# A hybrid encoder layer on one core: loads, waits, fills and closing sums put in another order

## The chip, the cores and the metric

The kernel runs on one core of one Trainium2 chip, as one program. The time is the device time of that core in microseconds (us), from start to end of one execution. Each engine (TensorE, ScalarE, VectorE, GpSimd, SyncE) runs its own list of instructions in order, and waits on semaphores that the others or the transfers raise. A matmul reads a stationary and a moving operand from SBUF and writes to PSUM.

## The reference

One layer (DEPTH = 1) is applied to a prompt of 256 rows and a sample of 1024 rows, with D_MODEL = 1024. All is float32.

```python
def run_trunk(x, ...):
    x = x + token_mixer(rmsnorm(x, norm_mix[l]), ...)
    x = x + expert_choice_ffn(rmsnorm(x, norm_ffn[l]), w_router[l], w_gate[l], w_up[l], w_down[l])
    return rmsnorm(x, norm_final)
# token_mixer: proj = hn @ w_in; a depthwise convolution over 5 rows, SiLU and an L2 norm on the
# first 3*512 columns feed a gated delta rule in both directions; the next ones feed windowed
# attention; both are gated, summed and multiplied by w_out.
# expert_choice_ffn: each of 16 experts takes its top T/8 rows (by affinity) and computes
    hdn = silu(xe @ w_gate) * (xe @ w_up)
    y[idx] += (hdn @ w_down) * gate
```

An expert thus takes 128 sample rows and 32 prompt rows, and the last result is an RMS norm of all rows.

## The kernel before, in words

The 1280 rows are ten tiles of 128 rows. Products that need precision are made of three matmuls: both factors are split into a rounded part and a rest (`rest`, line 78), and rounded x rounded, rounded x rest and rest x rounded are added. The work goes through phases, with a barrier of all engines between two. The change touches three of them.

**`phase_norm`, 0 to 40 us.** SyncE loads the ten x tiles (line 162), the gain and the identity, and the first two of 24 blocks of w_in, "weights 0" and "weights 1" (`load_weights`, line 159), all on one queue. For each tile ScalarE squares and sums (`square`, line 180), VectorE and ScalarE make 1/rms, VectorE scales (`normalise`, line 224), TensorE transposes eight squares of 128 into `px` (line 268), ScalarE rounds these (line 189) and VectorE makes the rest (line 78). Between the transposes TensorE already multiplies weights 0 with rows 0 to 511 and then 512 to 1023 (`first_rows`, line 85: 24 matmuls each). The tiles of x lie in `tk_stage_second` (the first three) and `xall`.

**`phase_channels`, from 41 us.** For each block c of w_in VectorE splits the weights (`split`, line 539), TensorE makes three products for rows 0 to 511, 512 to 1023 and the prompt (`project`, line 85, into `ch_wide` and `ch_tail`), ScalarE copies them into `raw` (line 461), VectorE convolves (five instructions, lines 559 and 562), ScalarE takes SiLU and the square (lines 486 and 490), and TensorE sums the squares by head (`head_sums`, line 423). GpSimd first fills the padding columns of `raw`, `rn` and `perm` with zero; ScalarE waits for all of these fills and for three small constants before its first copy. `perm` is a part of `tk_stage_second`.

**`phase_experts`, from 1438 us.** GpSimd gathers an expert's 128 sample rows into `xs` (line 2843) and, for four experts at a time, the prompt rows into `xp` (line 2848). TensorE transposes them, ScalarE and VectorE split them (`round_x`, `rest_x`). An expert's weights are 12 pieces of 1 MB, n = 0 to 11: eight for gate and up, four for down. SyncE loads piece i = 12 e + n into place i mod 10 (line 2822); the places 0 to 7 are held in `weights`, 8 and 9 in `ex_weights`, and the pieces 0 to 7 were loaded in the phase before. TensorE raises `used` by four after every fourth piece, and that sets when a place may be loaded again. ScalarE rounds each piece (`round_weights`, line 2994) and VectorE makes its rest, three pieces ahead of TensorE. After four pieces half of the hidden columns are there: SiLU (lines 3009 and 3013), a product on VectorE (3102, 3104), transposes (2954, 2959), and the split (3017, 3019, 78). `final_square(t)` (line 3033) sums the squares of a tile of x2, the rows before the last expert is added, `final_inverse` and `final_root` (3113, 3037) make 1/rms for two tiles, `final_scale` (3121) scales them, and SyncE writes them (2835). The x2 tiles are loaded two at a time (line 2832) into places 2 to 6 as these come free. At the end the rows of the last expert are written over (line 2875). The last expert is LAST_E = 15, so its pieces are i = 180 to 191.

The order in every engine's list is the order of the Python code: loops over e and n with calls at fixed n.

## Time and profile before

| | |
|---|---|
| median of three runs | 2210.48 us (2209.83 to 2215.64) |
| the profiled execution | 2215.64 us, span 2213.9 us |
| TensorE busy | 2105.7 us, 95% |
| VectorE, ScalarE, GpSimd busy | 1325.9, 934.0, 581.4 us |
| mean granted TensorE clock | 0.978 of full |
| transfers | 469.81 MB, mean 212 GB/s |

The profiled execution is the slowest of the three, 5.2 us above the median. Starts in the rows below are counted from the start of its span. PE is TensorE, PEld its loading of stationary operands, DVE is VectorE, ACT is ScalarE, POOL is GpSimd, SP is SyncE. A bracket at the end of a row names how long the engine had been idle and what released it.

### The profile page before, as it was taken

Reading aid. Unit: us, or ns where it says so; the run is one execution under the profiler, and the core shown is the slowest. Engines: PE = TensorE matmul, PEld = TensorE weight load, DVE = VectorE, ACT = ScalarE, POOL = GpSimd, SP = SyncE. Lnnn points to the kernel's source line nnn. Section 1 sums busy time; section 2 is a strip of 40 time slices with the busy share of each in tenths; the row PEclk is TensorE's granted clock in tenths of the full one; section 3 lists DMA queues with packets and bytes.
Section 4 is the critical chain, followed back from the end, with each engine's and each line's share of the span. In section 5 each row is a group of like instructions: output and inputs, shape, how many; then the busy total and the mean of one; then the engine's idle time right before and its main releaser. Section 6 shows DMA issues by size and latency. Waiting matters only on the chain. (4 is left out here: it accounts for less than half of the span.)

```text
span 2213.9 us, 42214 instructions
## 1 busy us (share of the span) xinstructions
PE 2105.7 (95%) x17446; PEld 1719.1 (78%) x17446; DVE 1325.9 (60%) x1539; ACT 934.0 (42%) x1325; POOL 581.4 (26%) x584
## 2 busy tenths in 40 slices
PE   7999999999999998888889999899999999999996
PEld 6878888999999997677765666777777777777774
DVE  6556412025675647744549658866666767666675
ACT  5665411001111107721246443266565655656654
POOL 0000000003578656933337222111111111111111
PEclk9999999999999999998889999999999999999998
DMA  3333522139888768968965441457887878878787
GB/s 136 100 99 99 156 93 98 68 108 250 230 235 225 205 172 249 273 166 230 242 209 193 163 148 58 191 225 290 303 309 288 320 276 313 313 279 324 281 296 274
DMA packets 269488, 469.81 MB, mean 212 GB/s; under 512 B 152272, under 2 KB 194896, under 8 KB 242192
## 3 DMA queue, kind: packets, MB, share of 16 engines
q1 hardware_dynamic: 187760, 396.02, 52.6%
q0 software_dynamic: 15296, 48.32, 7.4%
q10 hardware_dynamic: 66272, 23.21, 4.4%
q8 instruction: 116, 1.90, 0.3%
q14 instruction: 44, 0.36, 0.1%
HBM read 363.90 MB, written 107.49 MB: 213 GB/s over the span
## 5 line engine op out<-in xcount | busy, mean ns | idle before, releaser
L78 DVE TENSOR_TENSOR ex_w_rest<-weights,ex_w_rounded 128x2048 fp32r<-128x2048 f32 x154 | 347.2, 2289 | 119.0 <-ACT ex_w_rounded L2994 117.8
L2994 ACT CAST ex_w_rounded<-weights 128x2048 fp32r<-128x2048 f32 x154 | 287.1, 1908 | 14.7 <-PEq L48 14.1
L2889 PE MATMUL ex_s_acc<-ex_w_rounded,ex_xt 128*128 128x512 f32 x1024 | 289.7, 396 | 2.7 <-DVE ex_w_rest L78 2.1
L2889 PEld LDWEIGHTS ex_s_acc<-ex_w_rounded,ex_xt 128*128 128x128 f32 x1024 | 189.0, 189 | 53.0 <-issue 13.6
L2889 PE MATMUL ex_s_acc<-ex_w_rest,ex_xt 128*128 128x512 f32 x512 | 158.6, 391 | 0.0
L85 PE MATMUL ch_wide<-normed,ch_w_rounded 128*128 128x512 f32 x384 | 154.0, 401 | 2.8 <-DVE normed_rest L78 1.3
L85 PE MATMUL ch_wide<-normed,ch_w_rest 128*128 128x512 f32 x384 | 152.1, 396 | 0.0
L85 PE MATMUL ch_wide<-normed_rest,ch_w_rounded 128*128 128x512 f32 x384 | 152.0, 396 | 0.0
L2889 PE MATMUL ex_y_acc<-ex_w_rounded,ex_ht 128*128 128x512 f32 x512 | 147.6, 399 | 0.7 <-DVE ex_ht L78 0.7
L2843 POOL DMA_INDIRECT ex_xs<-hn,rt_sample_idx x16 | 21.4, 1339 | 478.0 <-PE ex_s_acc L2934 454.0
L85 PE MATMUL tk_acc<-tk_w_rounded_first,normed 128*128 128x336 f32 x400 | 127.7, 319 | 1.6 <-PEq L48 1.6
L85 PE MATMUL tk_acc<-tk_w_rounded,normed 128*128 128x336 f32 x400 | 127.8, 319 | 0.0
L85 PE MATMUL tk_acc<-tk_w_rounded,normed_rest 128*128 128x336 f32 x400 | 126.8, 317 | 0.0
L85 PE MATMUL tk_acc<-tk_w_rounded_first,normed_rest 128*128 128x336 f32 x400 | 126.8, 317 | 0.0
L85 PE MATMUL tk_acc<-tk_w_rest_first,normed 128*128 128x336 f32 x400 | 126.6, 316 | 0.0
L85 PE MATMUL tk_acc<-tk_w_rest,normed 128*128 128x336 f32 x400 | 126.5, 316 | 0.0
L2889 PEld LDWEIGHTS ex_s_acc<-ex_w_rest,ex_xt 128*128 128x128 f32 x512 | 96.4, 188 | 20.8
L2889 PEld LDWEIGHTS ex_y_acc<-ex_w_rounded,ex_ht 128*128 128x128 f32 x512 | 92.5, 188 | 20.2 <-issue 1.5
L539 DVE CAST ch_w_rounded<-ch_w 128x1024 fp32r<-128x1024 f32 x22 | 15.3, 694 | 154.0 <-PE ch_tail L85 99.9
L78 DVE TENSOR_TENSOR ex_w_rest<-ex_weights,ex_w_rounded 128x2048 fp32r<-128x2048 f32 x38 | 86.4, 2289 | 30.1 <-ACT ex_w_rounded L2994 29.5
L2910 PE MATMUL ex_p_acc<-weights,ex_xpt 128*32 128x256 f32 x1664 | 96.3, 381 | 0.0
L85 PEld LDWEIGHTS ch_wide<-normed,ch_w_rounded 128*128 128x128 f32 x384 | 72.5, 189 | 19.2 <-issue 1.9
(427 smaller groups left out, 4647.9 us busy)
## 6 DMA issues: line engine op xcount, KB each, us to landing
weights<-in_w_expert SPq DMA_DIRECT2D x154, 1024.0 KB, 9.1
ex_weights<-in_w_expert SPq DMA_DIRECT2D x38, 1024.0 KB, 9.0
tk_w<-in_w_tok SPq DMA_DIRECT2D x10, 1344.0 KB, 7.2
ch_w<-in_w_ch SPq DMA_DIRECT2D x24, 512.0 KB, 4.5
sc_rows<-rows SPq DMA_DIRECT2D x40, 256.0 KB, 5.5
sc_qk<-qkv_ch SPq DMA_DIRECT2D x40, 256.0 KB, 6.3
laq<-sc_laq ACTq DMA_DIRECT2D x80, 128.0 KB, 3.6
dl_kv<-qkv_tok SPq DMA_DIRECT2D x40, 256.0 KB, 4.1
```

The source lines that it names most:

```text
L78: return dve.tensor_tensor(out, whole, rounded.bitcast(F32), ALU.subtract)
L85: mm = pe.matmul(out, stationary[a], moving[b], start=(first and n == 0), stop=(last and n == len(pairs) - 1))
L539: dve.tensor_copy(w_hi[:, b], wbuf[:, b]).then_inc(w_rounded, 1)
L2843: pool.indirect_dma_start(out=xs[:], out_offset=None, in_=dr["hn"], in_offset=bass.IndirectOffsetOnAxis(ap=sample_idx[:, e:e + 1], axis=0) ...
L2889: mm = pe.matmul(banks[:, b], x[:, k, x_part], w[:, i % SPLIT, kk, 512 * b:512 * b + 512], start=(k == 0 and x_part == 0 and w is w_hi), s ...
L2910: mm = pe.matmul(out, x, raw(i)[:, kk, q * QUARTER:(q + 1) * QUARTER], start=(k == 0), stop=(k == KT - 1), skip_group_check=True)
L2994: act.copy(w_hi[:, i % SPLIT], raw(i)).then_inc(w_rounded, 1)
```

## The change

There are three groups of edits. In `phase_norm` weights 0 are loaded before x tile 3, weights 1 are no longer rounded and split there, and the three steps (nine matmuls) of weights 0 with rows 512 to 1023 that stood before the last tile's transposes stand with the others after them. In `phase_channels` GpSimd fills the buffers as a whole, VectorE splits weights 1 as its first work, and ScalarE waits for four fills. In `phase_experts` SyncE doesn't wait for the gathers before it loads pieces 8 and 9; the first x is split between pieces 0 and 1; the final gains are loaded after the last piece; and the closing squares, roots and scalings stand at other places of the last expert.

```diff
--- before.py
+++ after.py
@@ -163,7 +163,7 @@
                     if t == 0:
                         sp.dma_start(gain[:], io["norm_mix"].partition_broadcast(P)).then_inc(const_in, 16)
                         sp.dma_start(ident[:], io["ident"]).then_inc(const_in, 16)
-                    if t == 3:
+                    if t == 2:
                         load_weights(0)
                 load_weights(1)
 
@@ -205,8 +205,6 @@
                         act.copy(weights.rounded[:, 0], weights.whole[:, 0]).then_inc(weights.rounded_done, 1)
                 for t in range(NT - 3, NT):
                     round_tile(t)
-                act.wait_ge(weights.loaded[1], 16)
-                act.copy(weights.rounded[:, 1], weights.whole[:, 1]).then_inc(weights.rounded_done, 1)
                 act.wait_ge(root_loaded, 1)
 
             @block.vector
@@ -243,8 +241,6 @@
                     if t == 2:
                         dve.wait_ge(weights.rounded_done, 1)
                         rest(dve, weights.rest[:, 0], weights.whole[:, 0], weights.rounded[:, 0]).then_inc(weights.split_done, 1)
-                dve.wait_ge(weights.rounded_done, 2)
-                rest(dve, weights.rest[:, 1], weights.whole[:, 1], weights.rounded[:, 1]).then_inc(weights.split_done, 1)
 
             @block.tensor
             def _(pe):
@@ -255,11 +251,7 @@
                         mm.then_inc(weights.proj_done, 1)
 
                 pe.wait_ge(const_in, 32)
-                AHEAD = 3
                 for t in range(NT):
-                    if t == NT - 1:
-                        pe.wait_ge(rest_done, 4 * CHUNK_TILES)
-                        first_rows(1, range(AHEAD))
                     pe.wait_ge(xn_done, t + 1)
                     for h in range(2):
                         if t >= 2:
@@ -272,7 +264,8 @@
                         pe.wait_ge(rest_done, 2 * CHUNK_TILES)
                     if CHUNK_TILES <= t < 2 * CHUNK_TILES:
                         first_rows(0, range(2 * (t - CHUNK_TILES), 2 * (t - CHUNK_TILES) + 2))
-                first_rows(1, range(AHEAD, KT))
+                pe.wait_ge(rest_done, 4 * CHUNK_TILES)
+                first_rows(1, range(KT))
 
 
 CH_TILES = 24
@@ -364,12 +357,10 @@
 
             @block.gpsimd
             def _(pool):
-                for at in (0, TS + 2, RAW - 2):
-                    pool.memset(raw[:, :, at:at + 2], 0.0).then_inc(pads_ready, 1)
+                pool.memset(raw[:], 0.0).then_inc(pads_ready, 1)
+                pool.memset(rn[:], 0.0).then_inc(pads_ready, 1)
                 pool.memset(eps[:], EPS).then_inc(pads_ready, 1)
-                pool.memset(rn[:, TS:TS + 2], 0.0).then_inc(pads_ready, 1)
-                for at in (0, PAD + TS, QK_COLS - PAD):
-                    pool.memset(perm[:, :, at:at + PAD], 0.0).then_inc(pads_ready, 1)
+                pool.memset(perm[:], 0.0).then_inc(pads_ready, 1)
 
                 def store(c, b, i):
                     pool.wait_ge(tok_done, 3 * c + 3)
@@ -448,7 +439,7 @@
 
             @block.scalar
             def _(act):
-                act.wait_ge(pads_ready, 8)
+                act.wait_ge(pads_ready, 4)
                 act.wait_ge(const_ready, 48)
 
                 def evacuate(c, b, j):
@@ -569,6 +560,7 @@
                     if not early(c, 1):
                         normalise(c - 1, 1 - b, i - (1 - b))
                     convolve(c, b, range(2, CONV))
+                split(1, 1, 0)
                 dve.wait_ge(const_ready, 48)
                 walk(dve, A_TILES, 4, tile)
                 split(A_TILES + 1, 1, A_TILES // 2)
@@ -2742,6 +2734,7 @@
 LAST_E = EXPERTS - 1
 FINAL_SLOTS = NT // 2
 FINAL_FIRST = 2
+FINAL_SQUARES = {6: (0, 1), 7: (2, 3), 10: (4, 5), 11: (6, 7, 8, 9)}
 
 
 def phase_experts(nc, io, dr, ident, held, w_loaded, routing, y):
@@ -2814,18 +2807,15 @@
         with nc.Block() as block:
             @block.sync
             def _(sp):
-                sp.wait_ge(gathered, 16)
-                sp.wait_ge(prompt_gathered, 16)
                 for i in range(HELD, NP * EXPERTS):
                     if i >= PLACES:
                         sp.wait_ge(used, i - PLACES + 1)
                     sp.dma_start(place(i), io["w_expert"][i // NP, i % NP]).then_inc(w_in[i % PLACES], 16)
-                    if i == at(LAST_E - 2, 0):
-                        sp.wait_ge(xp_turned, GANGS)
-                        sp.dma_start(fgain[:], io["norm_final"].partition_broadcast(P)).then_inc(fn_gain_in, 16)
-                        for q in range(QUARTERS):
-                            sp.dma_start(quarter_gain[q * CAP_P:(q + 1) * CAP_P], io["norm_final"][:, q * QUARTER:(q + 1) * QUARTER].partition_broadcast(CAP_P)).then_inc(fn_gain_in, 16)
-
+
+                sp.wait_ge(xp_turned, GANGS)
+                sp.dma_start(fgain[:], io["norm_final"].partition_broadcast(P)).then_inc(fn_gain_in, 16)
+                for q in range(QUARTERS):
+                    sp.dma_start(quarter_gain[q * CAP_P:(q + 1) * CAP_P], io["norm_final"][:, q * QUARTER:(q + 1) * QUARTER].partition_broadcast(CAP_P)).then_inc(fn_gain_in, 16)
                 sp.wait_ge(scattered, 32 * LAST_E)
                 for k in range(FINAL_SLOTS):
                     sp.wait_ge(used, NP * EXPERTS - PLACES + k + 1)
@@ -3007,8 +2997,6 @@
                         act.wait_ge(h_s, 2 * e + f)
                         act.wait_ge(h_p, 2 * e + f)
                     act.activation(sg[:], hidden(f, 0), ACT.Silu).then_inc(silu_s, 1)
-                    if (e, f) == (LAST_E, 1):
-                        final_square(0)
                     act.wait_ge(used, at(e, HALF_TILES * (f + 1)))
                     act.activation(sgp[:], p_acc[:, f, 0], ACT.Silu).then_inc(silu_p, 1)
 
@@ -3041,8 +3029,8 @@
                     act.activation(ss[:, 2, NT + n:NT + n + 1], ss[:, 1, NT + n:NT + n + 1], ACT.Sqrt).then_inc(rows_rstd, 1)
 
                 round_weights(0)
+                round_x(0)
                 round_weights(1)
-                round_x(0)
                 take_prompt(0)
                 for i in range(2, AHEAD):
                     round_weights(i)
@@ -3059,15 +3047,16 @@
                         if n == 10 and e + 1 < EXPERTS:
                             round_x(e + 1)
                         round_weights(at(e, n) + AHEAD)
-                        if e == LAST_E and n == 8:
-                            for t in (1, 2, 3):
+                        if e == LAST_E and n == 11:
+                            final_root(2)
+                        if e == LAST_E:
+                            for t in FINAL_SQUARES.get(n, ()):
                                 final_square(t)
-                for k in range(2):
-                    final_root(k)
-                for k in range(2, FINAL_SLOTS):
-                    final_square(H * k)
-                    final_square(H * k + 1)
-                    final_root(k)
+                        if e == LAST_E and n == 9:
+                            final_root(0)
+                            final_root(1)
+                final_root(3)
+                final_root(4)
                 act.wait_ge(fn_sumsq, NT)
                 act.wait_ge(yp_added, 1)
                 act.activation(squares[:, 0:QUARTER], yp[:], ACT.Square, accum_out=ss[:, 0, NT + 1:NT + 2]).then_inc(yp_squared, 1)
@@ -3132,8 +3121,8 @@
 
                 dve.tensor_reduce(fold[:], ident.rearrange("p (q j) -> p j q", q=QUARTERS), AX.X, ALU.add).then_inc(fn_folded, 1)
                 split_weights(0)
+                rest_x(0)
                 split_weights(1)
-                rest_x(0)
                 take_prompt(0)
                 for i in range(2, AHEAD):
                     split_weights(i)
@@ -3148,11 +3137,10 @@
                         if n == 10 and e + 1 < EXPERTS:
                             rest_x(e + 1)
                         split_weights(at(e, n) + AHEAD)
-                        if e == LAST_E and n == 8:
-                            final_inverse(0)
-                            final_inverse(1)
-                final_scale(0)
-                final_scale(1)
+                        if e == LAST_E and n in (8, 9):
+                            final_inverse(n - 8)
+                        if e == LAST_E and n in (9, 10):
+                            final_scale(n - 9)
                 final_inverse(2)
                 final_scale(2)
                 final_inverse(3)
```

The names in the rows below are the buffers; a row is one instruction, or several like it where it ends in x and a number. TensorE's list at the end of `phase_norm` before; of the nine matmuls only the first and of the fifteen behind the transposes the first stand here:

```order
L268 MATMUL px<-identity,xn 128x128 [waits p1_rest_done]
L268 MATMUL px<-identity,xn 128x128 x3
L85 MATMUL ch_wide<-normed,ch_w_rounded 128x512 [waits p1_rest_done]
...
L268 MATMUL px<-identity,xn 128x128 [waits p1_rest_done,p1_xn]
L268 MATMUL px<-identity,xn 128x128 x3
...
L85 MATMUL ch_wide<-normed,ch_w_rounded 128x512
```

and now:

```order
L260 MATMUL px<-identity,xn 128x128 [waits p1_rest_done,p1_xn]
L260 MATMUL px<-identity,xn 128x128 x3
L260 MATMUL px<-identity,xn 128x128 [waits p1_rest_done]
L260 MATMUL px<-identity,xn 128x128 x3
L85 MATMUL ch_wide<-normed,ch_w_rounded 128x512 [waits p1_rest_done]
```

All 24 matmuls now stand behind the last tile's transposes. GpSimd's list at the start of `phase_channels`, before and then now:

```order
L368 MEMSET ch_raw 128x2x2 x3
L369 MEMSET ch_eps 128x1
L370 MEMSET ch_rn 128x2
L372 MEMSET tk_stage_second 128x2x64 x3
```

```order
L360 MEMSET ch_raw 128x2572
L361 MEMSET ch_rn 128x1282
L362 MEMSET ch_eps 128x1
L363 MEMSET tk_stage_second 128x2944
```

The fills cover whole buffers in place of their edges. ScalarE's list in the last expert before, from the rounding of piece 189 on (the second name of an output, `fn_ss`, holds the sums; the semaphores have the names of their first users):

```order
L2994 CAST ex_w_rounded<-ex_weights 128x2048 [waits sc_capped,sc_prod_done]
L2994 CAST ex_w_rounded<-weights 128x2048 [waits sc_capped,p1_x_in2]
L3009 ACTIVATE ex_sg<-ex_s_acc 128x512 [waits at_v_loaded1,tk_last_stored,sc_capped]
L3033 ACTIVATE ex_xs,fn_ss<-weights 128x1024 [waits at_distance_loaded3]
L3013 ACTIVATE ex_sgp<-ex_p_acc 128x128 [waits sc_diff_done]
L2994 CAST ex_w_rounded<-weights 128x2048 [waits sc_capped,p1_x_in3]
L3033 ACTIVATE ex_xs,fn_ss<-weights 128x1024 [waits at_distance_loaded3,at_bias_act2]
L3033 ACTIVATE ex_xs,fn_ss<-weights 128x1024 [waits at_distance_loaded4,at_bias_act2] x2
L3017 CAST ex_ht<-ex_s_acc 128x4x128 [waits at_v_loaded2]
```

and now:

```order
L2984 CAST ex_w_rounded<-ex_weights 128x2048 [waits sc_capped,sc_prod_done]
L3021 ACTIVATE ex_xs,fn_ss<-weights 128x1024 [waits at_distance_loaded3]
L3021 ACTIVATE ex_xs,fn_ss<-weights 128x1024 [waits at_distance_loaded3,at_bias_act2]
L2984 CAST ex_w_rounded<-weights 128x2048 [waits sc_capped,p1_x_in2]
L3021 ACTIVATE ex_xs,fn_ss<-weights 128x1024 [waits at_distance_loaded4,at_bias_act2] x2
L2999 ACTIVATE ex_sg<-ex_s_acc 128x512 [waits at_v_loaded1,tk_last_stored,sc_capped]
L3001 ACTIVATE ex_sgp<-ex_p_acc 128x128 [waits sc_diff_done]
L2984 CAST ex_w_rounded<-weights 128x2048 [waits sc_capped,p1_x_in3]
L3005 CAST ex_ht<-ex_s_acc 128x4x128 [waits at_v_loaded2]
```

The squares of tiles 0 to 3, each of which waits for a load of x2, have moved ahead of the SiLU (2999, before 3009), two of them ahead of the rounding of piece 190.

## Rows read from the trace of the kernel before

**Rows 1.** The page: busy us by engine (share of the span) xinstructions.
```profile
PE 2105.7 (95%) x17446; PEld 1719.1 (78%) x17446; DVE 1325.9 (60%) x1539; ACT 934.0 (42%) x1325; POOL 581.4 (26%) x584
```

**Rows 2.** Timeline, first phase (start, us, engine, line); two transfers, us to landing.
```profile
3.22 0.44 SPq L162 DMA_DIRECT2D xall<-in_x  x1
3.71 0.54 SPq L159 DMA_DIRECT2D ch_w<-in_w_ch  x1
11.23 1.06 ACT L180 ACTIVATE sq<-xall 128x1024 f32<-128x1024 f32 x1
...
xall<-in_x SPq DMA_DIRECT2D x1, 512.0 KB, 7.6
...
ch_w<-in_w_ch SPq DMA_DIRECT2D x1, 512.0 KB, 8.3
```

**Rows 3.** Timeline, end of the first phase.
```profile
33.42 1.28 DVE L224 SCALAR_TENSOR_TENSOR xn<-xall,ss,gain 128x1024 f32<-128x1024 f32 x1
33.56 0.50 PE L85 MATMUL ch_wide<-normed,ch_w_rounded 128*128 128x512 f32 x1
...
38.45 1.22 DVE L78 TENSOR_TENSOR ch_w_rest<-ch_w,ch_w_rounded 128x1024 fp32r<-128x1024 f32 x1 [0.15 <-ACT ch_w_rounded L209]
```

**Rows 4.** GpSimd's fills (line L1462), ns min/median/max.
```profile
L1462 POOL MEMSET dc_room<- x3: 952/953/1206, 585.9 to 744.9; 128x1024 f32 x3
L1462 POOL MEMSET weights<- x1: 1806/1806/1806, 876.8 to 876.8; 128x2048 f32 x1
```

**Rows 5.** Timeline, start of the second phase.
```profile
41.11 0.17 POOL L368 MEMSET ch_raw<- 128x4 f32 x3 [40.13 <-POOLq L48]
...
44.11 1.08 ACT L461 COPY ch_raw<-ch_wide 128x512 f32<-128x512 f32 x2 [5.70 <-DMA ch_headsum<-in_headsum]
...
44.08 0.40 PE L85 MATMUL ch_wide<-normed,ch_w_rounded 128*128 128x512 f32 x1
...
55.60 1.96 PE L423 MATMUL ch_aux<-ch_sq,ch_headsum 128*128 128x512 f32 x4 [0.20 <-ACT ch_sq L490]
```

**Rows 6.** A VectorE cast beside GpSimd: timeline, and line L1298's durations.
```profile
584.22 1.97 DVE L1298 CAST tk_w_rounded<-tk_w 128x672 fp32r<-128x672 f32 x1
...
L1298 DVE CAST tk_w_rounded<-tk_w x20: 500/516/1971, 421.4 to 780.9; 128x672 fp32r<-128x672 f32 x20
```

**Rows 7.** Windows: busy us by engine, granted clock, DMA share, GB/s.
```profile
1455.00:1463.00 8.00, 7.59 (x32) 5.74 (x36) 8.00 (x5) 6.67 (x5) 0.00 (x0) 0.79 0.01 4
2160.00:2170.00 10.00, 10.00 (x65) 7.85 (x55) 6.06 (x5) 7.55 (x7) 3.80 (x2) 1.00 0.98 375
```

**Rows 8.** Entry into the experts: TensorE's timeline; the sixteen gathers (line L2843) to landing.
```profile
1450.36 0.71 PE L2889 MATMUL ex_s_acc<-ex_w_rounded,ex_xt 128*128 128x512 f32 x2
1455.41 0.74 PE L2889 MATMUL ex_s_acc<-ex_w_rounded,ex_xt 128*128 128x512 f32 x2 [2.07 <-DVE ex_w_rest L78]
...
DMA to landing us min/median/max: 4.4/6.6/8.0
```

**Rows 9.** SyncE's loads of x2 (line L2832): issue, first landing, all five.
```profile
2162.07 15.75 SPq L2832 DMA_DIRECT2D weights<-x  x5
...
weights<-x SPq DMA_DIRECT2D x1, 1024.0 KB, 10.9
...
DMA to landing us min/median/max: 5.0/9.1/13.9
```

**Rows 10.** Timeline of the last expert and the close: ScalarE and VectorE.
```profile
2165.16 3.74 ACT L2994 CAST ex_w_rounded<-ex_weights 128x2048 fp32r<-128x2048 f32 x2
...
2192.82 1.28 DVE L3163 SCALAR_TENSOR_TENSOR ex_ys<-ex_y_acc,rt_gain_s,ex_ys 128x1024 f32<-128x1024 f32 x1
...
2198.13 2.48 DVE L3121 SCALAR_TENSOR_TENSOR weights<-weights,fn_ss,ex_xp 128x1024 f32<-128x1024 f32 x2
```

**Rows 11.** TensorE's timeline there.
```profile
2176.31 0.66 PE L2954 MATMUL ex_s_acc<-identity,ex_h 128*128 128x128 f32 x4
2183.28 0.70 PE L2889 MATMUL ex_y_acc<-ex_w_rounded,ex_ht 128*128 128x512 f32 x2 [0.68 <-DVE ex_ht L78]
```

## The prediction

> **What bounds the kernel now.** I read the page's shares first, then the engines' rows in time at the three places that the change touches, then the transfers there. TensorE is busy for 2105.7 us, 95% of the span, VectorE for 60% and ScalarE for 42% [rows 1]. So a wait put ahead of TensorE counts in full, and work taken off the other engines counts only where TensorE or the closing writes wait for it. Those places are the first 60 us, the entry into the experts at 1438, and the last 50 us.
>
> **1. Weights 0 loaded ahead of x tile 3.** Before, tile 3 is issued at 3.22 and lands after 7.6 us, at 10.8; weights 0 are issued at 3.71 and land after 8.3, at 12.0 [rows 2]. The two change places, so tile 3 lands at about 12.0. ScalarE squares it at 11.23 now [rows 2], in a run of work without a gap on which VectorE and TensorE hang, so all three move by 12.05 - 11.23 = +0.8. The earlier weights help nothing: their rounding stands behind the same two tiles as before. Bounds 0 and 1.2 (the difference of the landings).
>
> **2. The end of the first phase.** Before, nine matmuls of columns 512 to 1023 start at 33.56 and cover the wait for the last normalised tile, whose row ends at 33.42 + 1.28 = 34.70 [rows 3]; its transposes come after the nine. Now TensorE stands from 33.56 to 34.75, and the nine come afterwards: +1.2. Taken off ScalarE and VectorE are the rounding and the rest of weights 1. The later ends at 38.45 + 1.22 = 39.67 [rows 3], while TensorE's matmuls fill the time up to the second phase at 41.11 [rows 5] and now run longer; so the two hide behind TensorE and return nothing.
>
> **3. The second phase: whole buffers filled.** Now ScalarE waits for fills of 2572, 1282 and 2944 elements. A fill of 1024 took 0.95 and one of 2048 took 1.81 [rows 4], 0.83 ns for each further element: 2.24 + 1.17 + 2.55 + 0.1 for the small one = 6.05. From 41.11 they end at 47.2, where ScalarE's first copy starts at 44.11 today, released by a transfer [rows 5]. That is 3.1 later. Behind that copy stand the other two, five convolution steps, SiLU and the square that TensorE waits for already (0.20 at 55.60) [rows 5]; there is no slack.
> VectorE now also makes weights 1 here (cast 0.69, rest 1.23). Rows show that these engines hold each other up: one VectorE cast took 1.97 against a median of 0.516, from 584.22 to 586.19, with GpSimd at work from its start, and the GpSimd fill issued at 585.9 inside it took 1.21 instead of 0.95 [rows 4, 6]. So the cast slips in after the first fill and costs the fills 0.65: ScalarE starts 3.7 late. Weights 1 are ready at 45.4, 1.2 after TensorE asks at 44.08; that is inside the same 3.7 (1.2 here, 2.5 at the head sums). Bounds: 3.1 without a clash; 5.1 if the cast waits for all fills (47.2 + 0.69 + 1.23 = 49.2 against 44.08, after which ScalarE's lateness is hidden). I take 3.7.
> The Trainium skill says in "SBUF — State Buffer", section "Who interferes with whom", that a VectorE cast in a two-port mode and GpSimd exclude each other for a whole instruction, whoever issues first going first. By that rule the clash must come, and the trace agrees (1.97 against 0.516); without the rule the term would be 3.1.
>
> **4. The clock after a stall.** After the 2.07 us wait that ended at 1455.41 [rows 8] the granted clock averaged 0.79 over 8 us [rows 7], part of it at the low level of 1.2 GHz: 8 x 0.21 = 1.7 lost. I charge 1.7 once for step 3. Bounds 0 and 3.
>
> **5. Entry into the experts.** SyncE no longer waits for the two gathers; the 2 MB for places 8 and 9 go out at 1438 and run beside the first gather. Of the sixteen gathers the quickest, of which the first is one, took 4.4 us; the median, with weight loads beside it, is 6.6, the longest 8.0 [rows 8]. The first stands on TensorE's path (transposes, split of x, first matmul): 6.6 - 4.4 = +2.2, bounds 0 and 3.6. The early loads return nothing: place 8 is first read near 1470. The swap of x with weights 1 costs nothing either: rounding 1 (1.9) then follows the split of x and its rest (2.3) ends at 1449.6, ahead of 1450.36, when TensorE's second piece starts [rows 8]. The cover is TensorE's first piece and the prompt's transposes; 0.8 of it is left.
> The Trainium skill says in "DMA: Bandwidth & Descriptors", section "Queues, rings and completion order", that each DMA engine takes turns between the queues packet by packet. By that rule alone the gather's 0.52 MB would move beside as much of the loads, 1.05 MB instead of 0.52 at 375 GB/s, +1.4 instead of +2.2 and 0.8 less in the sum; the trace gives the larger number (6.6 against 4.4), so it decides.
>
> **6. The last expert.** ScalarE now runs squares 0 to 3 ahead of the second SiLU instead of one right after it and three later. Square 0 needs x2 rows, whose load is issued at 2162.07 and lands 10.9 later, at 2173.0 [rows 9]; the final gains now go ahead of it, 0.655 MB at the 375 GB/s of that stretch [rows 7] = +1.7. ScalarE is ready for square 0 when the second cast of its pair is over, at 2168.9 [rows 10], and stands there. Then: load 2174.7; two squares, each 1.06 as in [rows 2] with its accumulator's read, 1.2, so 2177.1; a rounding, half of 3.74 [rows 10], 2179.0; the second load is there (2162.5 + 13.9 + 1.7 = 2178.1 [rows 9]); two squares 2181.4; SiLU and VectorE's product, 1.4 together, 2182.8. TensorE is ready to transpose that product at 2176.31 and waits 6.5. Its 0.7 wait at 2183.28 goes [rows 11]: +5.8 at its last matmul. After that the rest is shorter: from 2192.82 to the end of the last scaling, 2198.13 + 2.48 = 2200.61, it was 7.8 [rows 10]. With the squares done it is 1.3 + 0.4 + 2.5 + 0.6 + 2.5 = 7.3. So +5.3, and 1.7 for the clock as in step 4. Bounds for the whole: -5.0 (below) and +9.
>
> **Sum.** 0.8 + 1.2 + 3.7 + 1.7 + 2.2 + 5.3 + 1.7 = +16.6. The profiled execution took 2215.64 and would take 2232.2. It is the slowest of the three; on the median of 2210.48 it gives 2227.1, and I say 2227.
>
> **Rivals.**
> - The cast waits for all fills and the clock stays low longer. For it: the cast of 1.97; against: a gap between fills lets the cast in. +1.4 on step 3, up to +3 with the clock: 2229 to 2232. 14%.
> - No clock loss at either stall, gather as fast as alone. For it: the loads' bytes may fall behind the gather's, and each stall may be split in two; against: the dip after 2.07 and the median of 6.6. -1.7 - 1.7 - 2.2 = -5.6: 2221. 16%.
> - The first phases' delay is taken up later, since TensorE idles for 5% of the span [rows 1]. Against: the phases hand over through barriers, and everything inside one starts from them. Steps 1 to 4 back, -7.4: 2220. 8%.
> - The other side: the early squares relieve the close. Place: ScalarE between the two SiLUs. If x2 rows 0 to 3 were there by 2168.9, no stall comes and roots and scalings start early: -1.3 by the same order of rows. The most it can give is -5.0: after the last matmul (2192.1 without its wait) only the last rows' sum, their square, root and scalings remain, until 2197.2 instead of 2202.2 [rows 10]. With steps 1 to 5 at 9.6 that is +8.3 to +4.6: 2219 to 2215, at the low end no slower than the measurement can tell. Against: loads that land at 2173.0 today cannot be ready at 2168.9, being issued as late and queued behind more. 12%.
>
> **How the numbers follow.** The forecast, with 50%, is 2227, its own range 2221 to 2232. A measurement of this kernel tells about 0.3%, 6.6 us, from no change, so "same" ends at 2217.1. Below it lie half of the last rival, a fifth of the absorbing one: 7% same, 2% faster for what I have overlooked, 91% slower. The range is 2216 to 2234: down to the relief case, up to the long lock with both clock losses.
>
> **What would show it.** Step 1: the square of tile 3 near 12.05. Step 2: TensorE idle for 1.2 before the last transposes of the first phase. Step 3: fills of about 2.2, 1.2 and 2.6 us, the first ScalarE copy 6.5 or more after the phase's start (3.0 now), TensorE waiting for weights 1 and again at the head sums, 3.7 together. Step 5: a first gather of 6 to 7 us. Step 6: ScalarE idle for 5 to 6 us before the first square, then TensorE waiting about 6 us before the transposes of the second hidden half. Fills below 3 us in all, or a square 0 that starts without a wait, would make the prediction wrong.

## The result and the profile after

The changed kernel takes 2233.92 us in the median of four runs (2233.15 to 2240.05), the kernel before 2210.15 in the four beside them. The ratio is 1.0104, with a 95% interval of 1.0083 to 1.0126: slower, as forecast. The forecast of 2227 was 7 too low, and the range (2216 to 2234) holds the time by 0.08 us. That it does is luck: the eighteen runs of the changed kernel on record lie between 2227.56 and 2240.41, with a median of 2233.6. The profiled execution took 2230.47 us (span 2228.8), 14.8 more than the profiled one of before, or 14.9 by the spans.

The page after shows why shares don't answer here: against [rows 1], TensorE's busy time grew by 4.7 us only, and the rest of the 14.9 is waiting.

```profile
PE 2110.4 (95%) x17446; PEld 1725.5 (77%) x17446; DVE 1329.4 (60%) x1540; ACT 933.4 (42%) x1324; POOL 589.2 (26%) x580
```

So I cut the spans at marks of TensorE's and VectorE's timelines, the same in every kernel: A from 0 to the second phase's first matmul, B to the first head sums, C to the start of the attention, D to the start of the experts, E to the first prompt product (`ex_p_acc`), F to the second prompt product of the last expert, G to the end of the last matmul (`ex_y_acc`), H to the end of the last scaling. us:

| kernel | A | B | C | D | E | F | G | H |
|---|---|---|---|---|---|---|---|---|
| before | 41.16 | 14.44 | 780.94 | 601.42 | 24.77 | 709.99 | 20.05 | 7.84 |
| after | 42.34 | 17.89 | 781.09 | 599.72 | 28.38 | 709.98 | 29.25 | 6.91 |
| difference | +1.2 | +3.5 | +0.2 | -1.7 | +3.6 | 0.0 | +9.2 | -0.9 |

The differences add up to 15.0. F agrees within 0.01 in all fourteen profiles of this study, C within 2.8; D, in which nothing was edited, lies between 595.3 and 604.8 in thirteen and is the main source of the spread of times (35 runs of the kernel before lay between 2205.96 and 2222.64). A step of 1 to 4 us is therefore read from its stretch; the medians of whole runs can only confirm the sum.

**The start (A).** Timeline of after (start, us, engine, line; in brackets the idle time before and its releaser): the square of tile 3, the last tile's transposes and the first matmul of the second phase, to be held against [rows 2, 3]:

```profile
11.92 1.06 ACT L180 ACTIVATE sq<-xall 128x1024 f32<-128x1024 f32 x1 [0.93 <-DMA xall<-in_x]
...
34.79 1.09 PE L260 MATMUL px<-identity,xn 128*128 128x128 f32 x8 [1.14 <-DVE xn L222]
...
42.34 0.36 PE L85 MATMUL ch_tail<-normed,ch_w_rounded 128*128 128x256 f32 x1 [0.88 <-PEq L48]
```

Both predicted waits are there, 0.93 and 1.14.

**The second phase (B).** After, against [rows 4, 5]:

```profile
42.30 2.25 POOL L360 MEMSET ch_raw<- 128x2572 f32 x1 [41.31 <-POOLq L48]
42.34 2.75 DVE L530 CAST ch_w_rounded<-ch_w 128x1024 fp32r<-128x1024 f32 x1 [4.95 <-PEq L48]
44.48 1.71 POOL L361 MEMSET ch_rn<- 128x1282 f32 x1
46.13 0.10 POOL L362 MEMSET ch_eps<- 128x1 f32 x1
46.17 2.56 POOL L363 MEMSET tk_stage_second<- 128x2944 f32 x1
46.40 0.50 PE L85 MATMUL ch_wide<-normed,ch_w_rounded 128*128 128x512 f32 x1 [0.98 <-DVE ch_w_rest L78]
48.76 1.07 ACT L452 COPY ch_raw<-ch_wide 128x512 f32<-128x512 f32 x2 [12.21 <-POOL tk_stage_second L363]
...
60.23 2.39 PE L414 MATMUL ch_aux<-ch_sq,ch_headsum 128*128 128x512 f32 x6 [2.40 <-ACT ch_sq L481]
```

The cast, 0.69 without a fill beside it, takes 2.75: it ends only after the first fill has ended (44.55), and the second fill, which starts beside it, takes 1.71 where it needs 1.17 alone. ScalarE starts 6.5 after the phase's start instead of 3.0.

**The entry (E).** TensorE's first transposes of the experts, after; before they waited for nothing that a row shows:

```profile
1449.74 1.97 PE L2924 MATMUL ex_s_acc<-identity,ex_xs 128*128 128x128 f32 x8 [3.81 <-DMA ex_xs<-hn,rt_sample_idx]
```

**The close (G, H).** After: SyncE's issues, ScalarE, TensorE, and two windows (busy us, granted clock, DMA share, GB/s), against [rows 9 to 11]:

```profile
2168.69 0.43 SPq L2816 DMA_DIRECT2D ex_xp<-in_norm_final  x1
2169.16 2.19 SPq L2818 DMA_DIRECT2D fn_quarter_gain<-in_norm_final  x4
2171.47 13.04 SPq L2822 DMA_DIRECT2D weights<-x  x5
2182.91 1.06 ACT L3021 ACTIVATE ex_xs<-weights 128x1024 f32<-128x1024 f32 x1 [7.34 <-DMA weights<-x]
...
2189.16 0.58 ACT L2999 ACTIVATE ex_sg<-ex_s_acc 128x512 f32<-128x512 f32 x1
...
2190.52 1.12 PE L2944 MATMUL ex_s_acc<-identity,ex_h 128*128 128x128 f32 x4 [7.45 <-DVE ex_h L3091]
```

```profile
2184.00:2190.00 6.00, 0.00 (x0) 0.00 (x0) 2.52 (x2) 5.94 (x11) 0.00 (x0) 0.66 0.99 366
2190.00:2196.00 6.00, 5.48 (x15) 4.53 (x16) 4.03 (x8) 2.26 (x2) 0.00 (x0) 0.50 0.41 164
```

ScalarE stands 7.34 us for the first x2 load with the SiLU behind the squares; TensorE stands 7.45 and then works at the low level of the clock (0.50 of full, 1.2 GHz) for several us.

### The profile page after: what moved, and what is told of

Its sections match the earlier page's. It is cut to its first block and busy times, and to the rows that moved or that the text cites. A ratio compares the mean times of both kernels' runs of the same rounds, so it can differ in the third digit from the quotient of the medians.

```text
span 2228.8 us, 42209 instructions
## 1 busy us (share of the span) xinstructions
PE 2110.4 (95%) x17446; PEld 1725.5 (77%) x17446; DVE 1329.4 (60%) x1540; ACT 933.4 (42%) x1324; POOL 589.2 (26%) x580
```

## The experiments

Each is the kernel before with one part of the change, unless it says otherwise. Differences are against the kernel before in the table's stretches; whole times are medians of 8 to 12 runs beside 19 to 35 of the kernel before on the same chip, and three times are those of one execution.

**The fills alone.** 
```diff
-                for at in (0, TS + 2, RAW - 2):
-                    pool.memset(raw[:, :, at:at + 2], 0.0).then_inc(pads_ready, 1)
+                pool.memset(raw[:], 0.0).then_inc(pads_ready, 1)
...
-                act.wait_ge(pads_ready, 8)
+                act.wait_ge(pads_ready, 4)
```

> The kernel before with the whole-buffer fills alone. Theory (each stall ahead of TensorE counts once and in full): fills of 2.25, 1.1, 0.1 and 2.56 us, no VectorE cast beside them, ScalarE's first copy near 47.2 instead of 44.1, TensorE waits about 3.3 us at the head sums: +3.1 to +3.4 us. Rival (a stall of 3 us also costs clock): +5. Rival (the delay is taken up later in the run): +1 or less.

Measured: 2220.9 against 2215.03, ratio 1.0023 (1.0007 to 1.0038). B +2.9, all else as before:

```profile
58.39 2.39 PE L421 MATMUL ch_aux<-ch_sq,ch_headsum 128*128 128x512 f32 x6 [3.12 <-ACT ch_sq L488]
```

The 3.1 of late fills reach TensorE in full, and no clock is lost behind the wait: the window 60 to 64 shows 1.00.

**Without the gather waits.**

```diff
-                sp.wait_ge(gathered, 16)
-                sp.wait_ge(prompt_gathered, 16)
```

> The kernel before with SyncE's two waits for the gathers taken out, nothing else. Theory: the two loads of 1 MB share the queues' engines with the first gather, which takes 6.5 to 8 us instead of 4.5 as in the profile after; TensorE's first expert piece comes that much later: +2 to +3.6 us. Rival (the missing part of the +23.8, which the profiled pair shows only as +14.8, lies in this race of transfers, whose outcome differs from run to run): +6 to +12 us, with a wide spread of the single runs.

Measured: 2219.84 against 2215.03, ratio 1.0021 (1.0006 to 1.0037). E +4.3; TensorE waits 3.48 for the gather, 8.0 to landing instead of 4.5. The early pieces gave nothing back.

```profile
1445.16 1.97 PE L2932 MATMUL ex_s_acc<-identity,ex_xs 128*128 128x128 f32 x8 [3.48 <-DMA ex_xs<-hn,rt_sample_idx]
```

**The closing order alone** (roots and scalings as in the change too, gains where they were).

```diff
-                    if (e, f) == (LAST_E, 1):
-                        final_square(0)
...
-                        if e == LAST_E and n == 8:
-                            for t in (1, 2, 3):
+                            for t in FINAL_SQUARES.get(n, ()):
                                 final_square(t)
```

> The kernel before with the closing squares, roots and scalings in their new places; the final gains are still loaded in the middle. Theory: ScalarE stands before square 0 until the x2 load lands (2173.0, not the 3 us later of the profile after, since no gains are ahead of it), the second SiLU comes 6 us late, TensorE waits 4.5 to 5.5 us and loses 1.7 to 2.4 us of clock, its old wait of 0.7 goes and the rest is 0.5 shorter: +5 to +7 us. Rival (early squares relieve the close and the stall in the profile after came from the gains load): 0 to -1.3 us.

Measured: 2218.72 against 2215.03, ratio 1.0017 (1.0001 to 1.0034). G +4.5, H -0.9. Timeline and window:

```profile
2169.86 1.06 ACT L3032 ACTIVATE ex_xs<-weights 128x1024 f32<-128x1024 f32 x1 [3.93 <-DMA weights<-x]
...
2177.48 1.12 PE L2955 MATMUL ex_s_acc<-identity,ex_h 128*128 128x128 f32 x4 [4.07 <-DVE ex_h L3102]
```

```profile
2176.00:2180.00 4.00, 2.52 (x8) 2.24 (x9) 2.51 (x4) 3.22 (x6) 0.00 (x0) 0.60 1.03 420
```

So about half of the 8.3 of the close is the order of the squares, the rest comes with the late gains.

**The first phase alone** (all its edits, fills as before).

```diff
-                    if t == 3:
+                    if t == 2:
                         load_weights(0)
...
-                        first_rows(1, range(AHEAD))
...
+                first_rows(1, range(KT))
...
+                split(1, 1, 0)
```

> The kernel before with the first phase's edits alone: weights 0 ahead of x tile 3, weights 1 split by VectorE at the start of the second phase, the nine matmuls behind the last transposes; fills small. Theory: TensorE waits 1.2 us before the last transposes, tile 3 comes 0.7 later, and the clock rises earlier and gives 0.8 back as in the profile after: +1.2 us; weights 1 are ready 2 us after the phase starts, before TensorE asks. Rival (the later work shifts and adds in full): +2.0 us. Rival (the missing 9 us lie here): +6 or more.

Measured: 2218.58 against 2215.03, ratio 1.0016 (1.0002 to 1.0031). A 42.42, B as before: the phase starts 1.3 later than in the profile of before, and the split of weights 1 beside the small fills costs nothing.

**The closing order with the late gains.** The closing order above, and

```diff
-                    if i == at(LAST_E - 2, 0):
-                        sp.wait_ge(xp_turned, GANGS)
-                        sp.dma_start(fgain[:], ...)   # and the four of quarter_gain
+                sp.wait_ge(xp_turned, GANGS)          # behind the loop over the pieces
+                sp.dma_start(fgain[:], ...)
```

> The kernel before with the closing order of the change and with the final gains issued behind the last piece. In the closing order alone ScalarE stood 3.93 us before square 0 and TensorE 4.07 before the transposes of the second hidden half; in the whole change it was 7.34 and 7.45. Theory (SyncE's own time): in the trace of the change the five issues of the gains occupy SyncE from 2168.69 to 2171.35, and the x2 loads are issued 2.8 late for that. If that makes the difference, ScalarE waits 7.2 to 7.4 here, TensorE 7.4, and the time is 7.5 to 8.5 above the kernel before plus what the clock loses (1 to 2.4). Rival 1 (bytes, the step of the prediction): only 0.655 MB go ahead, +1.7, so the waits are 5.6 and 5.8. Rival 2: the difference came from the experts' start, which this kernel leaves as it was; then the waits stay at 3.9 and 4.1.

Measured: 2224.48 against 2214.68, ratio 1.0043 (1.0029 to 1.0056). G +9.4, H -0.9:

```profile
2175.01 1.06 ACT L3031 ACTIVATE ex_xs<-weights 128x1024 f32<-128x1024 f32 x1 [7.45 <-DMA weights<-x]
...
2182.61 1.11 PE L2954 MATMUL ex_s_acc<-identity,ex_h 128*128 128x128 f32 x4 [7.57 <-DVE ex_h L3101]
```

```profile
2180.00:2184.00 4.00, 1.39 (x6) 1.29 (x7) 2.51 (x4) 3.97 (x8) 0.00 (x0) 0.50 1.04 421
2184.00:2188.00 4.00, 4.00 (x11) 3.12 (x10) 3.19 (x6) 0.35 (x1) 0.00 (x0) 0.50 0.10 40
```

The late gains add 3.5 to the wait (7.57 against 4.07), with nothing of the rest of the change present, and 1.4 more goes with the clock. Whether SyncE's time or the bytes do it is not told yet.

**The gains issued by GpSimd.** The whole change, but the five loads stand in GpSimd's list behind its last gathers.

```diff
-                sp.dma_start(fgain[:], ...)    # and the four of quarter_gain, ahead of the x2 loads
+                pool.dma_start(fgain[:], ...)  # and the four of quarter_gain, behind base_gathered's
```

> The whole change, with the five loads of the final gains issued by GpSimd behind its last two gathers instead of by SyncE ahead of the x2 loads. Theory (SyncE's own time for the five issues made the x2 loads late): x2 is issued at once when the scatters are done, ScalarE waits 3.9 to 4.4 before square 0 and TensorE 4.1 to 4.6 before the second half's transposes, as where the gains stand early; the time falls 3 to 4 below the whole change's, to about 2230 (2227 against the 2215 that the kernel before takes here, plus less clock loss). Rival (the 0.655 MB of the gains, wherever they are issued, take their share of the transfers while x2 loads): waits of 5.6 to 6. Rival 2: the gains now land after the first scaling wants them and the close waits; then the last scaling ends later than 8 us after the last matmul.

Measured: 2228.76 against 2212.79 in 8 runs, ratio 1.0059 (1.0040 to 1.0078); its profiled execution was its slowest, 2241.74, with a D of 611.6 and an A of 43.39. Only its close is used here; its second phase comes back in step 4.

```profile
2181.50 15.75 SPq L2817 DMA_DIRECT2D weights<-x  x5
...
2185.83 0.63 POOL L2858 DMA_DIRECT2D ex_xp<-in_norm_final  x1
2186.42 2.10 POOL L2860 DMA_DIRECT2D fn_quarter_gain<-in_norm_final  x4
...
2194.70 1.06 ACT L3020 ACTIVATE ex_xs<-weights 128x1024 f32<-128x1024 f32 x1 [6.39 <-DMA weights<-x]
```

My theory, that SyncE's own 2.7 us made the loads late, falls. x2 is issued at once and ScalarE still waits 6.39. Of the 3.4 to 3.5 that late gains add, 2.5 remain (6.39 against 3.93) when only their transfer is left, beside x2. The other 1.0 goes with the issues ahead of x2, but that is not shown by itself: here the gains are not only issued by another engine, they also go out 4.3 us after the first x2 load and not ahead of it. The rival, sharing of the transfers, was right, and larger than its 1.7.

**Squares behind the SiLU.** The closing order with another table:

```diff
-FINAL_SQUARES = {6: (0, 1), 7: (2, 3), 10: (4, 5), 11: (6, 7, 8, 9)}
+FINAL_SQUARES = {8: (0, 1, 2, 3), 10: (4, 5), 11: (6, 7, 8, 9)}
```

> The kernel before with the closing order of the change, except that squares 0 to 3 stand behind the second SiLU, with n = 8, and not ahead of it; gains as before. Theory (the placement ahead of the SiLU is the whole cost of the closing order): ScalarE doesn't stand before the SiLU, TensorE has no wait of over 1 us before the second half's transposes, and the last scaling ends 7 to 8 after the last matmul; the time is that of the kernel before within 1 us, perhaps 0.5 less because root 0 and the first scalings come earlier. Rival: the roots and scalings that now stand between the last expert's steps hold ScalarE (a table load of 1.28) or VectorE ahead of TensorE's operands, and TensorE waits 1 to 3 in the last 15 us: 1 to 3 slower.

Measured: 2213.99 against 2214.68, ratio 0.9994 (0.9980 to 1.0009). G +1.2, H -0.8. No stall at the SiLU, and the clock stays at 1.00 to the end. The 1.2 are TensorE's wait for the cast of the hidden rows, which four squares now delay:

```profile
2186.52 0.70 PE L2890 MATMUL ex_y_acc<-ex_w_rounded,ex_ht 128*128 128x512 f32 x2 [1.86 <-DVE ex_ht L78]
```

So it is the place ahead of the SiLU, and not the roots and scalings, that costs. Behind the SiLU the new order is worth +0.4 in G and H together.

**Two and two**, an attempt at a kernel faster than both:

```diff
-FINAL_SQUARES = {8: (0, 1, 2, 3), 10: (4, 5), 11: (6, 7, 8, 9)}
+FINAL_SQUARES = {8: (0, 1), 9: (2, 3), 10: (4, 5), 11: (6, 7, 8, 9)}
```

> The kernel before with the closing order of the change, but squares 0 and 1 with n = 8, behind the second SiLU, and squares 2 and 3 with n = 9, behind the cast of the hidden rows. Before, one square ahead and three behind put that cast 0.68 late for TensorE; four with n = 8 made it 1.86 late. Theory: with two squares ahead of the cast it is there in time, TensorE's 0.68 goes, the last matmul of the first expert half follows without a gap, and the last scaling ends 0.5 to 1 earlier, counted from the start of the last experts' second half; by the time alone this is not to be told from the kernel before (0.3%). Rival: the wait only moves to the closing rows (squares 4 to 9 or root 2 late), and nothing is gained or 1 is lost.

Measured: 2215.01 against 2212.79, ratio 1.0007 (0.9994 to 1.0021). The theory's first half holds: TensorE's last wait is gone, G is -0.9. But H is +1.2, as the rival said:

```profile
2177.44 4.88 DVE L3121 SCALAR_TENSOR_TENSOR weights<-weights,fn_ss,ex_xp 128x1024 f32<-128x1024 f32 x4 [1.22 <-ACT fn_ss L3036]
...
2182.63 0.20 ACT L3036 ACTIVATE fn_ss<-fn_ss 128x2 f32<-128x2 f32 x1 [2.97 <-DVE fn_ss L3115]
...
2185.33 0.16 DVE L3113 TENSOR_SCALAR fn_ss<-fn_ss 128x2 f32<-128x2 f32 x1
...
2186.00 1.28 DVE L3162 SCALAR_TENSOR_TENSOR ex_ys<-ex_y_acc,rt_gain_s,ex_ys 128x1024 f32<-128x1024 f32 x1
```

Read as a chain: root 2 on ScalarE waits for VectorE's inverse 2, which stands behind four scalings (4.88); squares 6 and 7 stand behind root 2; VectorE's inverse 3 waits for them at 2185.33, and the last rows' sum stands behind it, 1.95 after the last matmul (2184.05). No version here beats the kernel before.

**First phase and fills together** (both diffs above).

> The kernel before with both the edits of the first phase (weights 1 split in the second) and the whole fills. Apart they moved the head sums from 55.60 to 56.90 and to 58.39. Theory (the cast slips between two fills): the first cast of VectorE takes about 2.75, the fill of ch_rn 1.7 instead of 1.17, TensorE waits about 1.0 for weights 1 and 2.4 at the head sums, which start at 60.2: 0.5 more than the two effects added. Rival 1 (no clash): the head sums start at 55.60 + 1.3 + 2.8 = 59.7 and the fill takes 1.17. Rival 2 (the clock falls after the stall, as the prediction charged): windows from 56 to 66 show less than full clock, 1.7 us more. Rival 3: part of the delay is taken up before the attention starts; then the start of the attention is less than 4.6 later. Time by the theory: about 5 above the kernel before.

Measured: 2221.09 against 2214.68, ratio 1.0027 (1.0011 to 1.0043). Head sums at 60.29, cast 2.75, second fill 1.71, B +3.45, as in the whole change to 0.01. The fills alone gave +2.9: the clash is worth 0.5. The clock is 1.00 from 44 to 72. The phase's start is 42.40.

**The first fill three times**, to make the stall longer.

```diff
+                for k in range(3):
+                    if k:
+                        pool.wait_ge(pads_ready, k)
+                    pool.memset(raw[:], 0.0).then_inc(pads_ready, 1)
```

> The kernel before with the whole fills, ch_raw filled three times. This asks whether a longer stall of TensorE in the second phase costs clock, which the prediction charged with 1.7. With the fill once, TensorE waited 3.1 at the head sums (58.39) and the granted clock stayed at 1.00. Fills end 2 x 2.24 later, ScalarE's first copy starts at 51.4, head sums at 62.9 after waits of about 7.6 in all. Theory 1 (here no stall costs clock): granted clock 1.00 from 56 to 70, head sums at 62.9. Theory 2 (a long enough stall does): a window behind the stall shows 0.5 to 0.9 and the attention starts more than 7.6 after that of the kernel before.

Measured in one execution: 2221.07. TensorE's wait and the windows behind it:

```profile
62.58 4.16 PE L424 MATMUL ch_aux<-ch_sq,ch_headsum 128*128 128x512 f32 x6 [7.72 <-ACT ch_sq L491]
```

```profile
56.00:60.00 4.00, 0.00 (x0) 0.00 (x0) 3.93 (x4) 0.15 (x1) 0.00 (x0) 0.91 0.00 0
60.00:64.00 4.00, 1.42 (x2) 0.84 (x3) 1.65 (x2) 3.95 (x4) 0.00 (x0) 0.50 0.00 0
64.00:68.00 4.00, 4.00 (x18) 2.50 (x16) 0.00 (x0) 1.43 (x3) 0.00 (x0) 0.73 0.01 4
```

At the same place a wait of 7.72 brings the clock down and one of 3.12 didn't, each in one execution. The six head sums behind it take 4.16 instead of 2.39: 1.8 lost there.

**One piece early.**

```diff
+                    if i == HELD + 1:
                         sp.wait_ge(gathered, 16)
                         sp.wait_ge(prompt_gathered, 16)
```

> The kernel before with only piece 8 (1.05 MB) loaded ahead of the gathers; piece 9 waits for them as before. Alone the first gather took 4.49 us to landing; with both pieces (2.1 MB) beside it 7.95, in two kernels. Theory (what delays it is the bytes of the loads that move before it ends, at the 410 to 416 GB/s of those stretches): 3.46 us are 1.43 MB of the 2.1; 0.67 MB had moved before the gather's own transfer began. With one piece 0.38 MB are left, so the gather takes 4.49 + 0.9 = 5.4 and TensorE waits about 1. Rival (any load of that queue beside the gather holds it up alike): 7 to 8 us as with two pieces. Rival 2 (half of the bytes, half of the price): 6.2.

Measured in one execution: 2215.2, E +1.1.

```profile
1442.93 1.10 PE L2935 MATMUL ex_s_acc<-identity,ex_xs 128*128 128x128 f32 x8 [1.16 <-DMA ex_xs<-hn,rt_sample_idx]
```

One piece costs 1.1 and two cost 3.6 to 4.3. In this one execution that fits the bytes still to move when the gather starts, and neither half of the price (2.2) nor a fixed one.

**Weights 0 ahead of tile 3, alone** (the first two lines of the first phase's diff).

> The kernel before with nothing but weights 0 loaded ahead of x tile 3. Where the granted clock of the first 41 us was 1.00, the second phase started at 40.4 to 40.6 (four profiles); where it was 0.96, at 41.0 to 41.2 (three); with all the edits of the first phase at 42.34 to 42.42, clock 1.00 (three). Theory (both steps of the prediction count in full): the square of tile 3 waits 0.7 to 0.9 for its load and the phase starts at 41.2 to 41.4 at full clock, or 41.8 to 42 with the dip. Rival: the delay of tile 3 is absorbed before the end of the phase, which then starts at 40.5 at full clock, and the 1.9 are all from the nine matmuls.

Measured in one execution: 2217.53, A 41.18 at a clock of 1.00, where the six unedited starts at 1.00 lie at 40.44 to 40.62: +0.65.

## Why the prediction was right, step by step

**1 and 2, predicted 0.8 and 1.2.** Right. Weights 0 alone give +0.65, all edits of the phase 42.34 to 42.42 in three profiles, +1.9 on the starts at full clock. The fourth with all the edits, the kernel whose gains GpSimd issues, starts at 43.39, also at a clock of 1.00; why it is 1.0 later is open. The pair of profiles shows only +1.2 because the one of before had a dip; the first 41 us of before and of after:

```profile
0.00:41.00 41.00, 26.19 (x128) 21.42 (x128) 28.40 (x44) 25.33 (x50) 0.31 (x5) 0.96 0.45 168
```

```profile
0.00:41.00 41.00, 26.07 (x127) 21.54 (x128) 27.07 (x43) 24.59 (x49) 0.31 (x5) 1.00 0.43 168
```

Of the nine profiles with this phase unedited, three have the dip and start the next at 41.03 to 41.23.

**3, predicted 3.7.** Right in place, order and size: fills 2.25, 1.71, 0.10 and 2.56, waits of 0.98 and 2.40, 3.5 in all. The clash, charged with 0.6, is 0.5, and the bound of 5.1 (cast behind all fills) did not come.
The rule of the Trainium skill, "SBUF — State Buffer", section "Who interferes with whom" (a VectorE operation in a two-port mode and GpSimd shut each other out for whole instructions), agrees with the 2.75 and the 1.71.

**4, predicted 1.7.** Wrong: it cost nothing. I carried the dip after 2.07 us at 1455 over to another place. Three profiles have the fills and the split of weights 1 together. In two the clock stays at 1.00. In the third, with the gains on GpSimd, the cast got in only after the second fill, TensorE waited 2.09 us for weights 1 and then worked at a lower clock:

```profile
43.39 3.86 DVE L530 CAST ch_w_rounded<-ch_w 128x1024 fp32r<-128x1024 f32 x1 [4.95 <-PEq L48]
48.57 0.79 PE L85 MATMUL ch_wide<-normed,ch_w_rounded 128*128 128x512 f32 x1 [2.09 <-DVE ch_w_rest L78]
```

```profile
48.00:52.00 4.00, 3.43 (x8) 2.76 (x9) 1.27 (x2) 1.35 (x3) 1.75 (x1) 0.57 0.00 0
```

Even there B is 17.96 against 17.89. Without the dip TensorE would only have stood longer at the head sums, whose time the late fills set; so the dip, where it came, was hidden. Only the stall of 7.72 lost about as much as I had charged (1.8).

A stall's length alone doesn't say whether the clock falls. The wait of 2.07 at the entry into the experts [rows 8] is in all fourteen profiles (2.04 to 2.07); over the 8 us behind it the clock averaged 0.79 in twelve [rows 7] and 1.00 in two, the change and "Two and two":

```profile
1463.73:1471.73 8.00, 8.00 (x68) 5.88 (x72) 8.00 (x4) 6.73 (x5) 0.00 (x0) 1.00 0.01 2
```

```profile
1449.26:1457.26 8.00, 8.00 (x68) 5.88 (x72) 8.00 (x4) 6.72 (x5) 0.00 (x0) 1.00 0.01 2
```

"Two and two" has the entry of the kernel before and an E of 23.52, where the nine others with that entry have 24.54 to 24.98. The dip there is worth 1.0 to 1.5.

**5, predicted 2.2.** Right mechanism, mis-sized term: 3.6 in the change, 4.3 alone, at and beyond my upper bound. I took the median of the sixteen gathers (6.6) where the longest (8.0) was the likeness. And the wait is not the whole of it. Before, TensorE had a short wait behind these transposes, which is gone where the gather is late:

```profile
1446.76 0.70 PE L2889 MATMUL ex_s_acc<-ex_w_rounded,ex_xt 128*128 128x512 f32 x2 [0.67 <-DVE ex_xt L78]
```

So the gather's wait adds 2.8 alone (3.48 less 0.67) and 3.1 in the change (3.81 less 0.67). The rest goes with the clock, for which I had charged nothing here: alone it is 1.5, with 0.61 in the window 1445 to 1449, where the kernel before has 1.00. In the change it is 0.5, with 0.50 from 1449 to 1453 and 0.70 from 1453 to 1457, but no dip behind the wait of 2.07. These two rests are what is left of E, not measured by themselves.

The wait of 3.48, at the 410 GB/s of 1441 to 1445 in that kernel, is 1.4 MB of the loads' 2.1.
The Trainium skill's rule of turns between queues ("DMA: Bandwidth & Descriptors", "Queues, rings and completion order"), read as equal turns in bytes, gave +1.4: too low. But packets differ in size. The queues from 1430 to 1460 in the kernel without the waits (packets, MB, share of the DMA engines):

```profile
q1 hardware_dynamic: 295, 2.14, 18.7%
q0 software_dynamic: 432, 1.57, 14.4%
```

The loads' are 7.3 KB, the gathers' 3.6. By turns packet for packet, 0.52 MB of gather pass beside 1.05 MB of loads, +2.5; an estimate from that page and these rows, if the profile's packets are the page's, that still falls 1 short.

**6, predicted 5.3 and 1.7 for the clock.** Right mechanism, 8.3 instead of 7.0. The wait was 7.45, not 6.5: of it 4.07 belong to the squares' place (6.5 less the gains' 1.7 is 4.8, so this part was charged too high), and 3.4 to the gains, charged with their bytes at 375 GB/s, 1.7. Measured, 2.5 of it remain when GpSimd issues them; the other 1.0 goes with SyncE's issues ahead of x2, which I had left out. The rest of G, 2.4 (+9.2, less the wait of 7.45, plus the old one of 0.68), goes with the clock. The relief rival's H of -1.3 was -0.9.

**The sum.** Predicted 16.6 on the profiled execution, measured 15.0: +1.2, +3.5, 0, +3.6, +8.3 and 0.2, less 1.7 in D, where nothing was changed. Too much on step 4, too little on 5 and 6, nearly cancelled. The forecast's last move was its worst: I took the profiled 2215.64 for a slow execution and went down to the median of three, 2210.48. The medians of 35, 29 and 19 runs are 2215.03, 2214.68 and 2212.79, so 2215.64 was ordinary; 2232 would have been the better number. The same luck of few runs makes the paired medians differ by 23.8 where the profiled pair differs by 14.8. Against the later medians the eighteen runs of the changed kernel are 18.5 to 20.8 slower; the stretches without D's -1.7 and the dip that the profile of before had in A give 17.3.

None of the rivals came as such. The cast that waits for all fills: it got in after the first in two profiles (2.75) and after the second in one (3.86), never after the last. The absorbed start: C would have to be 4 to 7 shorter and is 0.2 longer. No clock loss and an undisturbed gather: true for the clock of step 3, false for the gather and for the close. The relief: the squares did wait.

What stays open: why the clock fell after 2.07 us at 1455 and not after 3.12 at 58, nor after the same 2.07 in two other profiles; what lets the cast in after the first fill or after the second; what makes D differ by 9 us between executions (its granted clock from 841 to 1200 lay between 0.90 and 0.92 in the thirteen, 0.87 in the one with 611.6); and how the swap of x with weights 1 stands alone, which was not tried. What the three single executions say, and the split of the gains' price into transfer and issues, rests on one profile each.

## What to carry to other kernels

A load brought forward, or one put off to a busier moment, is paid for by the transfer that it now runs beside. Look for the next transfer that the critical engine waits for, and count the bytes that are still moving when it starts. Reductions that "fill a gap" cost little where they stood behind the instruction that TensorE waits for (0.4 here), and ahead of it they cost as long as their input is late (4.07 here, 7.45 with the gains). And take the spread of a stretch from several executions before correcting a sum by the median of three.

## What was not expected of the hardware

- Stalls of 2.40 and 3.12 us cost no clock; the same wait of 2.07 was followed by 0.79 in twelve profiles and by 1.00 in two; 4.07 ended in a window at 0.60, and 7.45 to 7.72 were followed by 0.50.
- The same code let VectorE's cast in after the first fill in two profiles (2.75 us) and after the second in a third (3.86 us), and the head sums came at the same time in all three, 17.89 to 17.96 us after the start of the phase.
- 0.655 MB of gains, issued by GpSimd while x2 loads, made x2 2.5 us later, and issued by SyncE ahead of x2 3.4 to 3.5, where their bytes at the measured rate are 1.7.
- A stretch of 600 us without edits varied by 9 us (and once by 16), while another of 710 us repeated to 0.01.
